# Where the expert rows of a decoder trunk are served: the planner's row shares moved between stages

## What is computed

```
h = RMSNorm(x);  z = h @ W_in
x += W_out( sum_i sigmoid(gate_i) * (branch_i @ W_branch_i) )      # diff attention, MLA, short convolution
x += PEER(RMSNorm(x))                                              # 8 heads x 16 of 16384 experts per token
x += sigmoid(RMSNorm(x) @ W_pg) * (p[layer] @ W_pp)                # "PLE"
```

```
act = gelu(einsum('thkd,td->thk', u_tab[expert], hc))
return einsum('thk,thkd->td', gate * act, v_tab[expert])
```

## Time and profile before

| | |
|---|---|
| median of 3 runs | 3770.04 us (3766.02 to 3770.3) |
| profiled execution | 3774.79 us |
| its span, first to last instruction | 3773.0 us |
| mean granted TensorE clock | 0.892 |
| rows of experts | 1024, of which 533 by TensorE and 491 by DVE |
| read from HBM | 1294.51 MB, 344 GB/s over the span |

### The profile page before, as it was taken

One profiled execution on the slowest core, in us unless ns is written; L12 is line 12 of the kernel. 1 busy time (PEld: TensorE's weight loads), 2 busy tenths in 40 slices (PEclk: granted clock), 3 DMA queues, 4 the chain that ended last, 5 costly groups with the idle time before them and its releaser, 6 DMA issues.

```text
span 3773.0 us, 28818 instructions
## 1 busy us (share of the span) xinstructions
PE 2929.2 (78%) x8156; PEld 1487.3 (39%) x8156; DVE 2485.5 (66%) x5160; ACT 1487.2 (39%) x4001; POOL 1332.5 (35%) x1033
## 2 busy tenths in 40 slices
PE   7689848777998788767989788867998885555556
PEld 4444714534436234433436234534436331111112
DVE  1221486776667876766658876776657877777774
ACT  2230224458433343457432343458433342222222
POOL 0000033333332443434333443334333445555551
PEclk9889978989999899988999898989999896777778
DMA  4214279889998999989998999889999999999994
GB/s 151 81 67 156 102 320 379 340 364 378 393 382 347 399 411 378 383 345 405 404 374 333 410 409 368 343 348 367 390 378 363 388 403 416 422 422 421 422 421 184
DMA packets 182399, 1298.53 MB, mean 344 GB/s; under 512 B 20320, under 2 KB 21856, under 8 KB 26592
## 3 DMA queue, kind: packets, MB, share of 16 engines
q0 software_dynamic: 147456, 1073.81, 70.6%
q1 hardware_dynamic: 34784, 222.88, 15.1%
HBM read 1294.51 MB, written 2.10 MB: 344 GB/s over the span
## 4 chain that ended last, share of the span: by engine, by line
PE 46%; DMA 21%; DVE 14%; ACT 13%; issue 5%; POOL 1%; SPq 0%; DVEq 0%; ACTq 0%; POOLq 0%
DMA ring<-in_uv,experts 16%; PE ps_sum L1299 12%; PE ps_act L1361 8%; PE ps_act L1533 8%; PE ps_act L1406 8%; DVE ring L1173 5%; DMA wt<-in_weights 4%; PE ps_dve L1361 3%; PE ps_dve L1561 2%; DVE x L1182 2%; ACT L750 2%; ACT L537 2%; ACT area_e L537 2%; ACT diag L758 2%; ACT weight L752 2%
## 5 line engine op out<-in xcount | busy, mean ns | idle before, releaser
L507 POOL DMA_INDIRECT ring<-in_uv,experts x1024 | 1330.0, 1299 | 2369.1 <-PE ps_sum L1299 926.5
L1299 PE MATMUL ps_sum<-ring,diag 128*128 128x512 f32 x2132 | 1240.1, 726 | 658.1 <-ACT diag L758 650.6
L1173 DVE SCALAR_TENSOR_TENSOR ring<-ring,h_ffn 128x1024 f32<-128x1024 f32 x1024 | 1233.8, 1220 | 197.9 <-DMA ring<-in_uv,experts 192.0
L1299 PEld LDWEIGHTS ps_sum<-ring,diag 128*128 128x128 f32 x2132 | 445.0, 223 | 1333.1 <-ACT diag L758 919.2
L1182 DVE SCALAR_TENSOR_TENSOR x<-ring,weight,x 128x1024 f32<-128x1024 f32 x491 | 629.4, 1282 | 213.3 <-ACT weight L752 212.9
L750 ACT ACTIVATE dots<-dots 128x1 f32<-128x1 f32 x1024 | 205.3, 201 | 1333.3 <-DVE ring L1173 1331.7
L1406 PE MATMUL ps_act<-area_h,wt 128*128 128x256 f32 x1536 | 348.6, 386 | 2.5 <-ACT area_h L523 2.5
L1533 PE MATMUL ps_act<-wt,area_h 128*128 128x512 f32 x768 | 338.6, 596 | 10.0 <-DMA wt<-in_weights 9.8
L1361 PE MATMUL ps_act<-wt,area_h 128*128 128x512 f32 (+1 forms) x768 | 331.6, 592 | 5.2 <-ACT area_h L523 5.1
L1406 PEld LDWEIGHTS ps_act<-area_h,wt 128*128 128x128 f32 x1536 | 296.2, 194 | 54.6 <-issue 11.0
L752 ACT ACTIVATE weight<-dots,gate 128x1 f32<-128x1 f32 x1024 | 301.6, 295 | 34.1
(11 more groups left out here) (171 smaller groups left out, 2047.7 us busy)
## 6 DMA issues: line engine op xcount, KB each, us to landing
wt<-in_weights SPq DMA_DIRECT2D x192, 1024.0 KB
ring<-in_uv,experts POOLq DMA_INDIRECT x1024
wt<-in_weights SPq DMA_DIRECT2D x12, 512.0 KB
wt<-in_weights SPq DMA_DIRECT2D x4, 768.0 KB
x<-in_x SPq DMA_DIRECT2D x4, 512.0 KB, 5.0
area_y<-in_keys SPq DMA_DIRECT2D x4, 512.0 KB, 9.5
area_f<-in_keys SPq DMA_DIRECT2D x4, 512.0 KB, 10.7
area_f<-in_ffn_rows SPq DMA_DIRECT2D x4, 512.0 KB, 4.0
```

Of the source, the lines that this page charges most:

```text
L507: pool.indirect_dma_start(ring[:, row.slot, :], None, a[f"uv{row.step // 2}"][:, :], bass.IndirectOffsetOnAxis(ap=experts[:, row.step % 2, ...
L1173: dve.scalar_tensor_tensor(u, u, 1.0, h_ffn[:, row.tile, :], ALU.mult, ALU.mult, accum_out=dots[:, row.j:row.j + 1]).then_inc(dots_ready, 1)
L1299: ins = pe.matmul(ps_sum[:, b, :], diag[:, row.pe_before % DIAGS, :], ring[:, row.slot, D + b * 512:D + (b + 1) * 512], start=row.pe_first ...
```

## The change

Nothing of what is computed changes, and no instruction's shape. Two tables of the planner do:

```diff
 ROWS_IN = {
-    "ple_norm": 4, "ple_out": 6, "x_norm": 4, "qkv": 4.5, "latent": 4, "conv_c": 2.2, "conv_x": 2.2, "conv_b": 2.2, "taps": 1,
-    "diff_sq": 1, "diff_norm": 1, "diff_turn": 1.5, "diff_scores": 0.8, "diff_flip": 0.8, "diff_pv": 0.4, "diff_sub": 2,
+    "ple_norm": 4, "ple_out": 5, "x_norm": 4, "qkv": 3.7, "latent": 4, "conv_c": 2.2, "conv_x": 2.2, "conv_b": 2.2, "taps": 1,
+    "diff_sq": 1, "diff_norm": 1, "diff_turn": 1.5, "diff_scores": 1, "diff_flip": 1, "diff_pv": 0.4, "diff_sub": 2,
     "mla_norm": 5, "mla_up": 5, "mla_sums": 4, "mla_qk": 3, "mla_rope": 4, "mla_turn": 4, "mla_scores": 1, "mla_flip": 0.8,
-    "mla_pv": 0.5, "mla_out": 1.5, "gate_a": 1.7, "gate_b": 1.7, "branch_first": 1.6, "branch_more": 1.6, "mix_turn": 2,
-    "out": 3.5, "ffn_norm": 4, "query": 1.6, "scores": 0.5, "rank": 1.6, "topk": 3,
+    "mla_pv": 0.5, "mla_out": 1.5, "gate_a": 1.5, "gate_b": 1.5, "branch_first": 1.4, "branch_more": 1.4, "mix_turn": 2,
+    "out": 3, "ffn_norm": 4, "query": 2.1, "scores": 0.5, "rank": 1.9, "topk": 3,
 }
 PE_PART = {"ple_out": 0, "conv_c": 0, "conv_x": 0, "conv_b": 0, "qkv": 0, "latent": 0, "gate_a": 0, "gate_b": 0, "branch_first": 0, "branch_more": 0,
-           "out": 0, "query": 0.5, "scores": 0.5, "rank": 0.5, "topk": 1, "taps": 1, "diff_sq": 1, "diff_norm": 1,
+           "out": 0, "query": 0.6, "scores": 0.6, "rank": 0.6, "topk": 1, "taps": 1, "diff_sq": 1, "diff_norm": 1,
```

## The result

The changed kernel takes 3849.78 us (median of 4 runs, 3844.28 to 3857.29), and the kernel before, beside it on the same chip, 3770.17 us (3766.02 to 3771.51). The ratio is 1.0217, with a 95% interval of 1.0203 to 1.0231: 79.6 us slower. The forecast was 3802 us with a range of 3763 to 3828. The direction was right, and the size was less than half of what came.

A forecast was written before the change was run, and what follows sets the result against it. TensorE and DVE were taken to set the pace outside topk, where the DMA does. Terms of +10.9 us in step 0, +8.7 each in steps 1 and 2, +3.9 in step 3 sum to +32.2: 3802 us, range 3763 to 3828.

The forecast's parts named there:

- Queries: Query stages, steps 0 to 2: 6 or 7 more rows, all PE rows, cost +9.6 us a step; ends 0 and +21.2.
- rival 4: Much slower: PE rows of the queries stall the list, dot and matmul in turn; +35 us more, 3837 us, chance 0.08.
- Mix: Mix stage, four DVE rows fewer: only TensorE's waits for weights go, -3.3 us a step; ends 0 and -10.0.
- PLE: PLE stage, steps 1 and 2, two DVE rows fewer: -1.0 us a step; ends 0 and -5.0.
- ffn_norm: Norm stage, steps 1 and 2, one PE row fewer: -1.2 us a step; ends 0 and -3.1.
- The first rival: Faster: DMA sets the pace of PLE, qkv, mix and out, 2.49 us per row taken; 3738 us, chance 0.09.
- Step 3: Last step: PLE -1.0 us, two more rows in the stretch behind it +4.9, together +3.9.
- qkv and diff: Both stages together, two more PE rows priced at 1.88 us each: +3.8 us a step; ends 0 and +8.7.
- diff_sub: Stage diff_sub: one row turns from DVE to TensorE, +0.8 us a step; ends -1 and +2.
- MLA: MLA stages, priced with mix_turn: a PE row more or less, 0 us; ends -2 and +2.
- The line on POOL: POOL's gathers: POOL waits for slots, not its own issues, and gathers follow the rows; 0 by itself.
- rival 2: Slightly faster: idle time of queries and diff takes all that is put there; -10 us, 3760 us, chance 0.05.

The follow-up runs named there:

- late_in_rank: Kernel before with the changed kernel's mix-to-queries rows, one PLE row less, and query PE rows mostly put ahead of rank: 3775.98 us, ratio 1.0022.
- counts_only: Kernel before with only the changed row counts by stage (ROWS_IN), TensorE's shares (PE_PART) kept: 3843.38 us, ratio 1.0193.
- early_only: Kernel before with the changed kernel's qkv and diff words and fewer PLE rows, the rest as before: 3801.89 us, ratio 1.0094.
- mla_as_after: Kernel before with the changed kernel's words in diff_sub and MLA, both letters and slid rows: 3794.28 us, ratio 1.0063.
- mla_rot1_c: Kernel before with the sequence of PE and DVE rows in MLA turned by one row, every stage's count kept: 3791.83 us, ratio 1.0066.
- best: Kernel before, same counts, with diff's PE rows moved to convolution and latent stages and the queries' ahead of rank and scores: 3752.12 us, ratio 0.9954.
- placed: Changed kernel's counts outside MLA, PE rows moved to convolution and latent stages and mostly ahead of rank, diff_sub and MLA as before: 3778.88 us, ratio 1.0022.

## Why the prediction was right or wrong

- **Queries, +28.8 for +31.6: right in size, and only in part in the reason.** They take 120.5, 121.2 and 121.2 us, inside 117 to 124. TensorE is busy for 86% there. DVE is busy for 82% and not over 85%, as I said. I had priced five of the seven rows as dots on a full list of DVE, 5.8 of the 9.6 us. The head shown grew by one PE row of TensorE, 1.71 us, with DVE busy for 12.13 of its 14.54 us. So it is TensorE's order that pays, and the fit of the size is partly luck. The place is the other third, as late_in_rank shows. A PE row between ranking and scores was rival 4, which put the price on all of the added rows.
- **Mix, -9.9 for -10.7, PLE -2.0 for -2.2, ffn_norm -2.4 for -2.5: right.** The mix took 130.6 us in step 1, and PLE 51.8. TensorE's waits for weights in the mix, which I had priced, fell from 9.8 to 2.0 us, though step 0 gave 6.2 of the 10.7 us. At the end of PLE in step 1 DVE now waits 1.00 us for the second bank of L1383, as foreseen. In the chain of the changed kernel, step 1, qkv 0 and 1 have their 27.75 us as in the earlier trace rows:

```profile
1451.41 27.75 PE ps_act L1361 x64
```

- **The first rival fell.** It asked for 2.49 us per row taken. PLE gave 0.7 and 1.6 for two rows. In step 1 GB/s fell from 403 to 366 in PLE, from 404 to 351 in qkv and from 400 to 386 in the mix, and the stages hardly moved. The most that a stage gave was 6.2 us for four rows, in the mix of step 0, for the 10.0 asked. Their DMA shares of 0.98 to 0.99 had been no bound.
- **Step 3, +3.9 for +0.5.** PLE gave 1.7 and the stretch behind it took 2.2 of the 4.9 us. Its gathers ran at 421 GB/s as before. One profile tells this badly. Over all the profiled kernels the stretch took 654.7 to 659.2 us with 240 rows and 657.5 to 662.1 with 242, and the means are 3.7 apart, so the term was nearer than one pair says.
- **qkv and diff, +11.4 for +19.4: mis-sized in step 0.** Steps 1 and 2 came out at +2.2 and +1.9, under my +3.8. Step 0 came out at +15.3, above the +8.7 that I had as upper end. I had counted PE rows and priced each at 1.88 us. The groups above show 12.5 us of additional waiting for diagonals. counts_only says the same with other letters: its diff grew by 16.2 us in step 1 and 3.0 in step 2, with the same counts in both. A count can't tell the price of a PE row in diff. The letters of diff alone can't either: early_only has those of the changed kernel in step 1 and one row more in PLE, and its diff grew by 8.9 us for 3.4.
- **diff_sub, +2.4 for +7.5.** I took the difference of two durations, 0.8 us, with an end of +2. The stage grew by 2.4 to 2.7 in each step, so the upper end was passed too. The sum looked at diff_sub's own words, dP Pd to PP dP, which are worth 2.9 us by mla_as_after. What it missed is the new diff ahead of it, which brings 8.6 us with the old words.
- **MLA, 0 for +32.7: the step that failed.** The prediction says "a PE row more or less, 0. Ends: -2 and +2". It read the planner's table for counts alone. The same table gave the words, and 37 to 40 of the 56 words of MLA in a step had changed. I had not costed which row of a stage is TensorE's, though the earlier trace rows held 395.3 us of TensorE waiting for just those. mla_as_after shows that the words are worth 27 us by themselves, and mla_rot1_c that the letters are worth 24. The line on POOL, "gathers follow the rows", fell with it: which row holds a slot decides which gather is late.
- **The idle time of rival 2** was there in parts: +10.2 us were paid in the queries of step 1 for seven rows with some 3 us of work each. It wasn't enough to carry the change.
- **The clock.** In diff the granted clock went from 0.90 to 0.93 in step 1 and stayed at 0.89 in step 0. In MLA's norms, with less work in a longer stretch, it went from 0.84 to 0.80. The Trainium skill, "TensorE: Matmul & The Clock Gate", section "Part 1: The HAM clock gate (the "warmup" mystery)", has idleness lowering the clock, and these rows agree in direction. In MLA's heads of step 1, at 0.84 for 0.88, some 4 us of TensorE's busy time go with it. The mean over the span is 0.896 for 0.892, so the loss as a whole is not one of clock.

Two small readings were off: the sixth DMA digit of the earlier trace rows is a 7, and qkv's row has 404 GB/s and not up to 403. Neither enters the sum.

Taken together, the sum of the amounts, +32.2, stands close to the 27 us between best and placed. That is partly luck. Between those two the queries differ by 21.5 us for the 28.8 forecast, qkv and diff by -4.3 for +11.4, and diff_sub by 6.8 for 2.4. The list lacked one line: what the change does to the order of P and d behind the edit.

## What to carry to other kernels

When work is dealt out to in-order engines by a running sum, a change of one share re-deals everything behind it. Write out the dealt sequence of both versions and compare it word by word, before any price is put on a count. Price a moved piece by what stands beside it on each engine, and in a ring of n slots also by which item n places on it holds up. Set amount and place apart before one is blamed: here the place was worth more than the amounts, and improving it alone was the only edit whose gain stands clear of the noise.

## What the runs showed of the hardware

This core took 421 and 422 GB/s from HBM in gathers, in the changed kernel's topk and in its step 3 behind PLE, as the kernel before did. The Trainium skill, "Perfetto Trace Analysis", section "Roofline", says that a single active core can pull more than its share of 358 GB/s, up to some 435 by its 16 DMA engines. These rows agree with that, and not with the section that the prediction cited.

The DMA share of diff in step 1 rose from 0.93 to 0.98 when GB/s rose from 365 to 381, and in the mix it went from 0.99 to 0.97 while GB/s fell from 400 to 386. So a share of 0.97 to 0.99 goes with anything from 381 to 404 GB/s here, and a share close to 1 didn't mean that the stage waits for it.
